# First weight splits moved ahead of the norm, and the feed-forward residual moved behind the first pair

## The reference, cut to what matters

```python
for i in range(2):
    h = layer_norm(DN_ALPHA * h + 0.5 * swiglu(h, ffn_w1[i, 0], ffn_w3[i, 0], ffn_w2[i, 0]), ...)
    mix = conv_and_s5(h) if i % 2 == 0 else sparse_attention(h)
    h = layer_norm(DN_ALPHA * h + mix, ...)
    h = layer_norm(DN_ALPHA * h + 0.5 * swiglu(h, ffn_w1[i, 1], ffn_w3[i, 1], ffn_w2[i, 1]), ...)
    h = h + (p[i] @ ple_w_proj[i]) * sigmoid(h @ ple_w_gate[i])

def swiglu(x, w1, w3, w2):            # w1, w3: 1024 x 2816, w2: 2816 x 1024
    return (silu(x @ w1) * (x @ w3)) @ w2
```

## Time and profile before

| what | value |
| --- | --- |
| median of 3 runs | 2674.25 us (2669.77 to 2676.24) |
| the profiled execution's own time | 2674.83 us |
| its span, first to last instruction | 2672.8 us |
| mean granted clock of TensorE | 0.793 |
| busy: PE, PEld, DVE, ACT, POOL | 82%, 49%, 34%, 25%, 9% |

### The profile page before, as it was taken

The page is one execution under the profiler, slowest core; times in us unless marked ns, Lnnn a source line. Parts: engine busy times, 40 slices in busy tenths (PEclk is TensorE's granted clock), DMA queues, the critical chain, the costliest instruction groups (busy, mean ns, idle before and its releaser), DMA issues.

```text
span 2672.8 us, 33435 instructions
## 1 busy us (share of the span) xinstructions
PE 2198.5 (82%) x13558; PEld 1313.2 (49%) x13558; DVE 904.4 (34%) x1532; ACT 659.6 (25%) x1160; POOL 235.8 (9%) x232
## 2 busy tenths in 40 slices
PE   7997667776667776667677889999999999899998
PEld 5754222212222122222122278876788788776886
DVE  6543000000000000000000179575665666664664
ACT  4321000000000000000000055411654655544554
POOL 1010000000000000000000079142000000040000
PEclk9997765556665556665665699999999999899999
DMA  5035999999999999999999945521654354333540
GB/s 221 31 144 217 425 426 426 425 425 426 425 425 426 426 425 425 425 425 426 425 426 425 394 188 187 187 104 40 278 188 176 149 189 178 122 134 119 189 177 16
DMA packets 80432, 753.94 MB, mean 282 GB/s; under 512 B 9863, under 2 KB 10024, under 8 KB 16936
## 3 DMA queue, kind: packets, MB, share of 16 engines
q1 hardware_dynamic: 77736, 750.12, 68.7%
q10 hardware_dynamic: 2624, 2.84, 0.4%
HBM read 751.88 MB, written 1.05 MB: 282 GB/s over the span
## 4 chain that ended last, share of the span: by engine, by line
PE 49%; DMA 36%; SPq 6%; DVE 6%; issue 1%; ACT 1%; POOL 0%; DVEq 0%; POOLq 0%; PEldq 0%; ACTq 0%; PEld 0%
DMA ring<-in_w_gate 23%; PE ps L1431 12%; PE ps L1444 9%; PE ps L1433 6%; DMA ring<-in_w_up 6%; SPq L1119 4%; DMA ring<-in_w_down 4%; DMA work<-in_w_gate 4%; PE ps L1144 3%; SPq L1122 2%; PE ps L415 2%; PE ps L1939 2%; PE ps L2098 1%; PE ps L1727 1%; PE ps L1754 1%
## 5 line engine op out<-in xcount | busy, mean ns | idle before, releaser
L1144 PE MATMUL ps<-ring,arena 128*32 128x352 f32 x3072 | 473.5, 766 | 174.7 <-DMA ring<-in_w_gate 93.8
L1431 PE MATMUL ps<-hsplit,w 128*128 128x512 f32 x1408 | 500.9, 398 | 0.5 <-DVE hsplit L1536 0.5
L1433 PE MATMUL ps<-hsplit,w 128*128 128x256 f32 x1408 | 395.0, 281 | 0.0
L1144 PEld LDWEIGHTS ps<-ring,arena 128*32 128x32 f32 x3072 | 112.5, 154 | 525.5 <-DMA ring<-in_w_gate 189.3
L1186 ACT ACTIVATE arena<-ps 128x352 f32<-128x352 f32 x32 | 13.1, 461 | 1158.0 <-PE ps L1144 1158.0
L1431 PEld LDWEIGHTS ps<-hsplit,w 128*128 128x128 f32 x1408 | 264.5, 188 | 65.6 <-DVE hsplit L1536 1.1
L1197 DVE TENSOR_TENSOR arena<-arena,ps 128x352 f32<-128x352 f32 x32 | 15.2, 518 | 826.3 <-ACT arena L1186 826.3
L1433 PEld LDWEIGHTS ps<-hsplit,w 128*128 128x128 f32 x1408 | 265.9, 189 | 3.1
L1444 PE MATMUL ps<-w,hidsplit 128*128 128x512 f32 x1056 | 255.3, 391 | 0.0
L1509 DVE TENSOR_TENSOR w<-ring,w 128x1024 fp32r<-128x1024 f32 x176 | 225.4, 1284 | 28.4 <-ACT w L1467 28.2
L1444 PEld LDWEIGHTS ps<-w,hidsplit 128*128 128x128 f32 x1056 | 192.1, 188 | 40.8
(11 more groups left out here) (399 smaller groups left out, 2461.8 us busy)
## 6 DMA issues: line engine op xcount, KB each, us to landing
ring<-in_w_gate SPq DMA_DIRECT2D x96, 1408.0 KB, 34.6
ring<-in_w_up SPq DMA_DIRECT2D x96, 1408.0 KB, 34.4
ring<-in_ffn_w SPq DMA_DIRECT2D x88, 1536.0 KB, 6.5
work<-in_w_down SPq DMA_DIRECT2D x64, 1536.0 KB, 35.5
ring<-in_w_down SPq DMA_DIRECT2D x32, 1536.0 KB, 37.7
work<-in_w_up SPq DMA_DIRECT2D x32, 1408.0 KB, 34.7
work<-in_w_gate SPq DMA_DIRECT2D x32, 1408.0 KB, 34.8
ring<-in_w_down SPq DMA_DIRECT2D x32, 1024.0 KB, 36.7
```

What stands on the lines that cost most here:

```text
L1144: last = pe.matmul(k.ps[32 * g:32 * g + CAP, 2 * w + half, 0:FH], xe[:, kk, :], slot(k, base + n)[:, g * FG + half * FH:g * FG + (half + 1 ...
L1431: pe.matmul(k.ps[:, bank(c, w), :], k.w13[:, b, w, 0, kk, :], k.hsplit[:, :, kk, :], start=(kk == 0), stop=False, skip_group_check=True)
L1433: last = pe.matmul(k.ps[:, bank(c, w), 0:S], k.w13[:, b, w, 1, kk, :], k.hsplit[:, 0, kk, :], start=False, stop=(kk == DK - 1), skip_group ...
```

## The change

Each stage gets two hooks, `scalar_ahead` and `vector_ahead`, that hold its first weight splits. The norm object at the end of a stage knows the stage that follows and calls the hooks: `NormAndTurn` before its first instruction on ACT and on DVE, `experts_combine` before its root on ACT and after its scaling on DVE, and `ple` between its sigmoids and its end on ACT and between its products and its additions on DVE. `ffn` and `sparse_attention` hand over their first weight splits, `ple` the first two of eight. `conv_s5` has no such splits. In `ffn` the call of `residual` goes behind `pair(0)` on PE. The ring with eight slots now starts at slot 5 and not at slot 2. `conv_s5` has a wait on ACT for the four gate products in front of its norm, since the new splits overwrite what these read.

```diff
@@ Ring.slot_of
+        if n >= FIRST_NARROW + NARROW_USES:
+            return (n - FIRST_NARROW - NARROW_USES + NARROW) % SLOTS
         return n % SLOTS
@@ experts_combine
     def scalar(act):
+        turn.following.scalar_ahead(act)
         act.wait_ge(ms_ready, 3)
         act.activation(m[:, 2:4], m[:, 2:4], ACT.Sqrt).then_inc(root, 1)
...
+        turn.following.vector_ahead(dve)
         turn.vector(dve)
@@ NormAndTurn
     def scalar(self, act):
         k = self.k
+        self.following.scalar_ahead(act)
         for t in range(ST):
...
         step = k.vector_order.on(dve)
+        self.following.vector_ahead(dve)
@@ ffn
     def tensor(pe):
-        residual(k, pe, fix(k, "seed2"))
...
         pair(0)
+        residual(k, pe, fix(k, "seed2"))
...
+    def scalar_ahead(act):
+        for w in range(2):
+            split_high(act, 0, w)
...
             act.activation(k.hsplit[:, 0, kk, :], k.hT[:, kk, :], ACT.Copy).then_inc(h_high, 1)
-            if kk == 0:
-                pair_high(0, 0)
-                pair_high(0, 1)
...
+    def vector_ahead(dve):
+        for w in range(2):
+            split_low(dve, 0, w)
@@ conv_s5
+        act.wait_ge(q["ya_put"], 4)
         norm.scalar(act)
@@ ple
+    AHEAD = 2
...
+    def scalar_ahead(act):
+        for kk in range(AHEAD):
+            split_high(act, kk)
...
             act.activation(sig[:, i, :], k.ps[:, i, :], ACT.Sigmoid).then_inc(sig_put, 1)
+        following.scalar_ahead(act)
...
             dve.tensor_tensor(sig[:, i, :], sig[:, i, :], k.ps[:, 4 + i, :], ALU.mult).then_inc(part_put, 1)
+        following.vector_ahead(dve)
         for i in range(4):
@@ sparse_attention
+    def scalar_ahead(act):
+        high(act, 0)
+
+    def vector_ahead(dve):
+        lows(dve, 0, 0)
+        lows(dve, 0, 1)
@@ program
+        for stage, following in zip(stages[-1:] + more_stages, more_stages):
+            stage.norm.following = following
```

More of the change, by code:

```diff
@@ L1 @@
+import functools
 import math
@@ L1288, in vector @@
                                      op0=ALU.mult, op1=ALU.mult).then_inc(turn.x_put, 2)
+        turn.following.vector_ahead(dve)
         turn.vector(dve)
-    return Stage(tensor, scalar, vector)
+    return Stage(tensor, scalar, vector, norm=turn)
 class NormAndTurn:
@@ L1461, in tensor, with split_high @@
         norm.tensor(pe)
+    def split_high(act, c, w, e=0):
+        if w == 0:
+            act.wait_ge(k.ready(base + c), landed(c, e))
+        act.activation(k.w13[:, c % 2, w, 0], raw(c, w), ACT.Copy).then_inc(w13_high, 1)
+    def scalar_ahead(act):
+        for w in range(2):
+            split_high(act, 0, w)
     def scalar(act):
[L1464 to L1467, removed]
+        pair_high = functools.partial(split_high, act)
         def down_high(c, e=0):
@@ L1549, in vector @@
         norm.vector(dve)
-    return Stage(tensor, scalar, vector, beside and beside.gpsimd)
+    return Stage(tensor, scalar, vector, beside and beside.gpsimd, norm, (scalar_ahead, vector_ahead))
 def s5_small(k):
@@ L1903, in gpsimd, with __init__, scalar_ahead, vector_ahead @@
                 pool.tensor_tensor(part[:, 2 * n], part[:, 2 * n], phase, ALU.mult).then_inc(q["s_put"], 1)
-    return Stage(tensor, scalar, vector, gpsimd)
+    return Stage(tensor, scalar, vector, gpsimd, norm)
+class Following:
+    def __init__(self):
+        self.following = None
+    def scalar_ahead(self, act):
+        if self.following:
+            self.following.scalar_ahead(act)
+    def vector_ahead(self, dve):
+        if self.following:
+            self.following.vector_ahead(dve)
 def ple(k, u, base, out=None):
@@ L1922, in ple, with split_high, split_low @@
     p_sb = slot(k, n_proj)[:, 2 * D:2 * D + 2 * S].rearrange("p (k s) -> p k s", k=2)
+    following = Following()
+    AHEAD = 2
+    def split_high(act, kk):
+        if kk % 3 == 0:
+            act.wait_ge(k.ready(base + kk // 3), k.use.mark[base + kk // 3])
+        act.activation(w_parts(kk)[0], raw(kk), ACT.Copy).then_inc(w_high, 1)
+    def split_low(dve, kk):
+        dve.wait_ge(w_high, high_before + kk + 1)
+        dve.tensor_tensor(w_parts(kk)[1], raw(kk), w_parts(kk)[0].bitcast(F32), ALU.subtract).then_inc(w_split, 1)
+    def scalar_ahead(act):
+        for kk in range(AHEAD):
+            split_high(act, kk)
+    def vector_ahead(dve):
+        for kk in range(AHEAD):
+            split_low(dve, kk)
     def tensor(pe):
@@ L1958, in scalar @@
             act.activation(k.hsplit[:, 0, kk, :], k.hT[:, kk, :], ACT.Copy).then_inc(h_high, 1)
-            if kk % 3 == 0:
-                act.wait_ge(k.ready(base + kk // 3), k.use.mark[base + kk // 3])
-            act.activation(w_parts(kk)[0], raw(kk), ACT.Copy).then_inc(w_high, 1)
+            if kk >= AHEAD:
+                split_high(act, kk)
         for i in range(4):
@@ L1992, in vector @@
                                   ALU.add).then_inc(x_put, 1)
-    return Stage(tensor, scalar, vector)
+    return Stage(tensor, scalar, vector, norm=following, ahead=(scalar_ahead, vector_ahead))
 def sparse_attention(k, base, causal, positions):
@@ L2082, in sparse_attention, with high, lows, vector_ahead @@
     PAIR_BANK = (4, 5, 6, 7, 6)
+    def high(act, n):
+        act.wait_ge(k.ready(base + n), k.use.mark[base + n])
+        for half in range(2):
+            act.activation(w_part(n, 0)[:, rows(half)], by_chunk(slot(k, base + n), n)[:, rows(half)],
+                           ACT.Copy).then_inc(w_high, 1)
+    def lows(dve, n, half):
+        split_low(dve, n, half).then_inc(w_split, 1)
+    def scalar_ahead(act):
+        high(act, 0)
+    def vector_ahead(dve):
+        lows(dve, 0, 0)
+        lows(dve, 0, 1)
     def tensor(pe):
@@ L2204, in scalar @@
         act.dma_start(pos_i, positions).then_inc(q["loaded"], 16)
[L2206 to L2210, removed]
         PLACES = ((0, W + ID, pr, WIDE, 1.0), (W + ID, W + ID + IH, wi, 0, IH ** -0.5 * ID ** -0.5),
@@ L2241, in scalar @@
             act.activation(k.c_hT_high[:, kk, :], k.hT[:, kk, :], ACT.Copy).then_inc(h_high, 1)
-            if kk == 0:
-                high(0)
-        high(1)
+        high(act, 1)
         for n in range(2):
@@ L2248, in scalar @@
         copies(0)
-        high(2)
+        high(act, 2)
         copies(1)
-        high(3)
+        high(act, 3)
         for b in range(INDEX_TURNS):
@@ L2257, in scalar @@
         copies(2)
-        high(4)
+        high(act, 4)
         relus(0, 10)
@@ L2261, in scalar @@
         relus(10, 16)
-        high(5)
+        high(act, 5)
         copies(4)
@@ L2288, in vector @@
         step = k.vector_order.on(dve)
-        def lows(n, half):
-            split_low(dve, n, half).then_inc(w_split, 1)
         for kk in range(DK):
@@ L2296, in vector @@
                               ALU.subtract).then_inc(h_split, 1)
[L2297 to L2301, removed]
+        lows(dve, 1, 0)
+        lows(dve, 1, 1)
         dve.wait_ge(q["loaded"], 32)
@@ L2308, in vector @@
         dve.tensor_scalar(arg[:, 1], arg[:, 1], -1.0, math.pi / 2, ALU.mult, ALU.add).then_inc(q["sin_arg"], 2)
-        lows(2, 0)
-        lows(2, 1)
+        lows(dve, 2, 0)
+        lows(dve, 2, 1)
         dve.wait_ge(q["sin_done"], B["sin_done"] + 2)
@@ L2315, in vector @@
         dve.tensor_copy(ki2[:, :, ID:2 * ID], pr[:, :, WIDE + W:ROW]).then_inc(q["vector_put"], 1)
-        lows(3, 0)
-        lows(3, 1)
+        lows(dve, 3, 0)
+        lows(dve, 3, 1)
         for i in range(ST * IH):
@@ L2337, in vector @@
             if t == 0:
-                lows(5, 1)
+                lows(dve, 5, 1)
         step(dve.tensor_copy(keep[:, 0, P:S], causal_sb[:, 0, P:S]))
@@ L2390, in gpsimd @@
                                    ALU.mult).then_inc(q["p_put"], 1)
-    return Stage(tensor, scalar, vector, gpsimd)
+    return Stage(tensor, scalar, vector, gpsimd, norm, (scalar_ahead, vector_ahead))
 def second(k, t, base, out):
```

22 lines of the change are left out of this document (12 added, 10 removed).

## The result

| | before | after |
| --- | --- | --- |
| median of 8 runs each | 2672.89 us (2669.77 to 2677.41) | 2682.79 us (2680.40 to 2688.34) |
| the profiled execution's own time | 2674.83 us | 2680.40 us |
| its span | 2672.8 us | 2678.4 us |
| mean granted clock of TensorE | 0.793 | 0.792 |

The change makes the kernel slower: ratio 1.0034 [1.0024, 1.0044], which is +9.1 us on 2672.89, the two medians 9.9 us apart. The forecast was 2683.0 us and slower by just over 0.3%. The interval holds 0.3%, so which side of that line it is on is not settled; that it is slower is. One run of experiment 3 took 3214.64 us at a mean granted clock of 0.587, and the ratios leave it out.

What follows compares the result with a forecast made beforehand. PE was taken to bound the chain from 1531 us on, broken by norms and barriers where DVE and ACT lead. Terms -0.6 + 0.96 + 2.3 + 5.4 - 0.45 + 0.95 = +8.6 us gave 2682.9 us, range 2676.5 to 2686.5.

Steps and rivals of the forecast that it cites:

- What bounds it, and the residual: ffn starts: residual already hides the splits; behind pair 0, PE waits for the activation's piece, +0.70 ffn 0, +0.96 ffn 1.
- `experts_combine`: Before ffn 0: the root's table load moves ahead of its input, -1.28 us; low splits on DVE cost nothing.
- Splits in front of the statistics: Ends of ffn 1 and ffn 3: low splits delay the statistics, +1.15 us each; end of ffn 2, +1.8 us.
- ple 0 to ffn 2: Late additions and barrier +2.7 us, wait for the first piece 0.96, restart at 1.2 GHz 1.7; together +5.4 us.
- +1.5 to +1.8 by the windows, I take 1.7: Start of ffn 2: after a longer rest PE restarts at 1.2 GHz, costing 1.7 us, or 0 if the clock stays.
- ffn 3: +0.95: Start of ffn 3: PE waits 0.95 us for the activation's first piece; no clock change counted.
- The splits cost nothing there: conv_s5 to ffn 1 and sparse_attention to ffn 3: PE's output product covers the early splits, 0 us.
- The ring: Three ffn 1 loads no longer stand behind conv_s5's output weights; nothing waited for them, so no gain or cost.
- The first: Rival: the clock is lost at ffn 0 too, +1.8 us, total +10.4 or 2684.7 us; chance 0.20.
- The second: Rival: the clock stays at 2.4 GHz behind ple 0, total +6.9, 2681.1 us; chance 0.15.
- The third: Rival: pair 0 first wakes PE sooner at ffn 1, 2 and 3; total +3.6, 2677.9 us; chance 0.11.
- The fourth: Rival: faster by over 0.3%, needing splits in the path everywhere; all hidden gives only -4 us; faster given 0.03.

Runs made afterwards that it cites:

- experiment 3: The changed kernel with ffn 2 put back: its splits inside its stage, no hook at ple 0's end, its residual first; 2676.81 us, ratio 1.0006 to before.
- experiment 1: The kernel before with only the residual moved behind pair 0, first weight splits still behind the barrier; 2690.56 us, ratio 1.0059 to before.
- experiment 6: The changed kernel with four of ple's gate splits ahead of the norm instead of two; 2688.87 us, ratio 1.0048 to before.
- experiment 5: The changed kernel with 42 identity transposes that compute nothing on PE behind ple 0's transposes; 2679.82 us, ratio 1.0021 to before.
- experiment 2: The changed kernel with the residual back in front of pair 0, leaving the early splits alone; 2678.26 us, ratio 1.0009 to before.
- experiment 4: The kernel before with only the eight-slot ring starting at slot 5; ratio 0.9992 to before.
- experiment 10: The changed kernel with idle-time filler transposes on PE in experts_combine, the norms, ple 0 and sparse_attention's start; 2669.58 us, ratio 0.9977 to before.
- experiment 7: The kernel before with hooks only in experts_combine and, for sparse_attention, both highs and one low half; 2669.37 us, ratio 0.9977 to before.
- experiment 8: The kernel before with filler transposes on PE in the rests of experts_combine, the norms and sparse_attention's start; 2660.89 us, ratio 0.9950 to before.
- experiment 9: The kernel before with hooks at experts_combine and sparse_attention plus PE filler transposes, 14 instead of 28 at sparse_attention's start; 2658.70 us, ratio 0.9936 to before.

## Why the prediction was right

**What bounds it, and the residual: right.** The splits were hidden under the residual; experiment 1 shows what they cost without that cover, and the changed kernel waits for the piece as forecast at every ffn. Measured +0.85 in ffn 1 and +1.10 in ffn 3 for the predicted 0.96 and 0.95. In ffn 0 it was +1.01 for +0.70: the transposes in front took 3.67 us and not 3.35, since they begin earlier and the clock rises at the same relative time (14.9) in both executions, so more of them run at 1.2 GHz.

That the median itself, 2682.79, falls so near the forecast of 2683.0 is partly luck: the kernel before measured 2672.89 in these runs and not 2674.25, and the change is 9.1 us by the ratio and not 8.6.

**`experts_combine`: right.** The table load went to the front of its wait, -1.36 for -1.28, and the two lows on DVE delayed nothing. The Trainium skill gives about 2.66 us, drain included, for a change of tables in ScalarE: Activation LUTs, What ACT_TABLE_LOAD costs; the gain of 1.36 us is near that of the row (1.28), and not that of the section.

**Splits in front of the statistics: right.** +0.96 and +0.94 for 1.15 twice, +1.69 for 1.8, and experiment 6 shows the mechanism by doubling it. At the end of ffn 1 the statistics start 3.36 us after ACT's first high (2065.42 - 2062.06) where 3.44 was taken; the other tenth is that ACT is free 0.12 us earlier against the first down product (169.69 us behind it, 169.81 before).

**ple 0 to ffn 2: right in mechanism, the clock mis-sized.** The late barrier and piece came to +3.72 for 3.66. The term "+1.5 to +1.8 by the windows, I take 1.7" measured 2.5. It was read from ffn 1 and ffn 3 of before, where PE had 3.9 and 3.16 us at 1.2 GHz behind its start; in ffn 2 it now has 5.89. Experiment 3 isolates the boundary (6.8 to 7.5 us), experiment 5 the clock within it (2.7 us). By the earlier trace rows the clock rose at 1545.81 us and fell at 1876.91, where the prediction has 1545.7 and 1876.95; no term changes by it.

**ffn 3: a term was missing.** "ffn 3: +0.95" took the clock as unchanged. Its slow part behind PE's start grew from 3.16 to 6.07 us, +1.03. The prediction had put PE's rest there 0.95 us longer without asking what that does to the clock. In experiment 2, where the residual comes first, this window is only 0.08 us longer than before.

**`conv_s5`: "The splits cost nothing there" is right, but the stage came out 1.10 us shorter.** Both executions spent 10.2 us at 1.2 GHz in it, before in one piece (relative 209.5 to 219.7), after in two (209.5 to 216.3 and 284.6 to 288.0), and the second lies where it may cost less. Experiment 1 does not touch `conv_s5` at all, has its slow time there in two such pieces as well (214.9 to 221.7 and 290.0 to 293.4), and the stage is 0.88 us shorter. So the code of the change is not needed for it; that the place of the slow stretches is the cause is argued from these records. The ring is not the cause (experiment 4: -0.01 us for this stage). This term and the one missing in ffn 3 cancel, and so part of the closeness of 8.6 to 9.25 is luck.

**The rivals.** The first (the clock lost at ffn 0 too) did not happen in the changed kernel, whose window there has 1.00. It did in experiments 1, 6 and 10, with slow stretches at relative 6.7 to 23.7, 16.7 to 20.2 and 14.9 to 21.7. Of the four profiled executions that have the changed kernel's start of ffn 0, without fillers there (after, 3, 5 and 6), it was one. The second (the clock stays up behind ple 0) is refuted by the 0.50 of the window. The third (pair 0 in front wakes PE sooner) too: ffn 1 has 17.00 us against 16.79, ffn 3 17.53 against 16.50. The fourth, that the splits stood in the path everywhere, is refuted by experiment 2: taken alone they win nothing, and cost 2.4 us by its median ratio (0 to 4.8).

## What to carry to other kernels

Work moved ahead of a barrier is free only on an engine that idles there, and "idle on average" is not the question: the low splits had DVE to themselves under the residual, and were put in front of the statistics or additions on which the whole barrier hangs. Move such work only where a wait for it stands in the trace; two of seven places had one, and splits moved at those two alone made the kernel faster. And before moving TensorE's first work behind a wait, look at how long it has then rested: in ffn 2 the slow restart cost 2.5 us on top of the 3.7 by which PE started late.

## What the runs showed of the hardware that was not expected

**The slow clock is worth more than the whole change.** Time at 0.50 of the clock, in us, from the last weighted sums to the end, in the profiled executions:

| kernel | at 0.50 | changed part against before |
| --- | --- | --- |
| before | 65.5 | 0 |
| after | 81.9 | +9.25 |
| experiment 1 | 92.6 | +18.8 |
| experiment 2 | 80.6 | +4.7 |
| experiment 3 | 75.1 | +2.5 |
| experiment 4 | 64.9 | -0.7 |
| experiment 5 | 71.7 | +6.0 |
| experiment 6 | 101.6 | +17.4 |
| experiment 7 | 75.7 | -0.2 |
| experiment 8 | 11.2 | -13.2 |
| experiment 9 | 11.6 | -16.6 |
| experiment 10 | 29.2 | -2.2 |

In experiment 8, 280 transposes that compute nothing, in rests that PE had anyway, took away 54 of 65.5 us at 1.2 GHz and 13.4 us of time.

**Transposes held the clock.** In the changed kernel the clock is still 1.00 in PE's rest before ffn 2 and 0.50 in the 5.89 us behind it. In experiment 5 that rest is filled by 4.72 us of nothing but transposes in float32, and the 14.76 us behind them run at 1.00. In the earlier trace rows the clock even rose to full among transposes alone, behind a rest of 6.70 us. The Trainium skill says in TensorE: Matmul & The Clock Gate, Part 4: PE-mode transpose, that transposes don't count as busy in the way that brings the full clock. For the transposes of this kernel the windows say otherwise, and they decide; the trace lists them as MATMUL and does not show whether they use the mode of which the section speaks.

**A small gain can move the later slow stretches.** In the profiled executions a microsecond won or lost at one place goes with slow stretches that begin elsewhere or last longer, and these cost or give some microseconds more: `conv_s5` gained 1.10 us that nobody forecast, and experiment 7's execution lost from ple 0 on what its two places had won, though its median is 6 us ahead. One profiled execution says where the time goes; for a total of a few us it takes the medians.
